# State-space layer: the skip term by ScalarE and an identity product, a modulation unit in halves about the input products

## The reference, cut to what matters

```python
u = (xn @ w_in).astype(jnp.float32)
...
y = (jnp.einsum('ghp,blgp->blgh', c_re.astype(jnp.float32), xr)
     - jnp.einsum('ghp,blgp->blgh', c_im.astype(jnp.float32), xi))
y = y.reshape(B, L, D_MODEL) + d_skip.astype(jnp.float32) * u
hg = jax.nn.gelu(y).astype(xn.dtype) @ w_glu
```

## Time and profile before

| | us |
|---|---|
| median of 3 runs | 1801.25 |
| lowest, highest | 1799.35, 1802.07 |
| the profiled execution, its own time | 1802.3 |
| its span in the trace | 1800.5 |
| clock granted to TensorE, mean | 0.978 |

### The profile page before, as it was taken

How to read it: one execution, slowest core, us unless ns; L and a number is a source line. 1 busy time by engine, 2 the same in 40 slices (tenths; PEclk the granted TensorE clock), 3 DMA queues, 4 the chain that set the end, 5 groups by cost and what they waited for, 6 DMA issues and landing times.

```text
span 1800.5 us, 34542 instructions
## 1 busy us (share of the span) xinstructions
PE 1689.0 (94%) x14415; PEld 1600.2 (89%) x14429; DVE 1238.5 (69%) x1567; ACT 844.9 (47%) x964; POOL 156.1 (9%) x128
## 2 busy tenths in 40 slices
PE   6999999998899997799999999999999999989997
PEld 6979999898899985599999897999998658889997
DVE  5847777786887757867777784777776667555454
ACT  5355545546445441245555535555544633343343
POOL 1002000103920043100000100200000000000000
PEclk9999999899999989999999999999999999999999
DMA  7804545535345531353554680445452032044551
GB/s 297 333 13 164 178 181 183 188 133 187 141 173 177 186 118 72 142 209 142 183 184 182 230 334 19 167 173 188 175 187 94 24 117 94 25 156 174 185 184 70
DMA packets 40050, 286.50 MB, mean 159 GB/s; under 512 B 4576, under 2 KB 4576, under 8 KB 5664
## 3 DMA queue, kind: packets, MB, share of 16 engines
q1 hardware_dynamic: 39024, 280.99, 43.1%
q10 hardware_dynamic: 944, 4.33, 0.6%
HBM read 284.25 MB, written 1.05 MB: 158 GB/s over the span
## 4 chain that ended last, share of the span: by engine, by line
PE 65%; DVE 17%; ACT 9%; issue 6%; POOL 1%; DMA 1%; DVEq 0%; ACTq 0%; POOLq 0%; SPq 0%
PE PS L1770 19%; PE PS L1771 19%; PE PS L1772 19%; ACT whi L386 5%; DVE wlo L928 4%; DVE AR L1153 4%; ACT AR L498 1%; DVE AR L1264 1%; DVE AR L1261 1%; ACT AR L589 1%; ACT AR L591 1%; DVE XL L972 1%; PE PS L2374 1%; POOL AR L2533 1%; DVE AR L1139 1%
## 5 line engine op out<-in xcount | busy, mean ns | idle before, releaser
L1770 PE MATMUL PS<-XH,whi 128*128 128x256 f32 (+1 forms) x2696 | 787.6, 292 | 46.8 <-DVE wlo L928 35.0
L1771 PE MATMUL PS<-XL,whi 128*128 128x256 f32 (+1 forms) x2696 | 778.4, 289 | 0.0
L1772 PE MATMUL PS<-XH,wlo 128*128 128x256 f32 (+1 forms) x2696 | 778.0, 289 | 0.0
L928 DVE TENSOR_TENSOR wlo<-raw,whi 128x2048 fp32r<-128x2048 f32 x240 | 557.3, 2325 | 180.7 <-ACT whi L386 180.6
L1770 PEld LDWEIGHTS PS<-XH,whi 128*128 128x128 f32 x2696 | 522.0, 194 | 60.6 <-issue 29.5
L1771 PEld LDWEIGHTS PS<-XL,whi 128*128 128x128 f32 x2696 | 522.7, 194 | 4.4 <-issue 0.2
L1772 PEld LDWEIGHTS PS<-XH,wlo 128*128 128x128 f32 x2696 | 522.5, 194 | 4.2
L386 ACT ACTIVATE whi<-raw 128x2048 fp32r<-128x2048 f32 x240 | 456.0, 1902 | 72.4 <-PE PS L1772 47.9
L1770 PE MATMUL PS<-HH,whi 128*128 128x256 f32 x880 | 250.7, 285 | 13.0 <-DVE HL L1173 8.5
L1772 PE MATMUL PS<-HH,wlo 128*128 128x256 f32 x880 | 249.7, 284 | 0.0
L1771 PE MATMUL PS<-HL,whi 128*128 128x256 f32 x880 | 249.7, 284 | 0.0
(11 more groups left out here) (365 smaller groups left out, 1522.5 us busy)
## 6 DMA issues: line engine op xcount, KB each, us to landing
raw<-wst SPq DMA_DIRECT2D x248, 1024.0 KB, 4.8
AR<-mst SPq DMA_DIRECT2D x17, 1024.0 KB, 5.5
XT<-x_in SPq DMA_DIRECT2D x2, 512.0 KB, 6.2
AR<-crow ACTq DMA_DIRECT2D x2, 512.0 KB, 5.7
AR<-sbc ACTq DMA_DIRECT2D x1, 1024.0 KB, 5.8
AR<-ctxin ACTq DMA_DIRECT2D x1, 1024.0 KB, 5.6
y_out<-XT SPq DMA_DIRECT2D x1, 1024.0 KB, 3.9
AR<-sgw ACTq DMA_DIRECT2D x1, 512.0 KB, 3.6
```

The source lines that it names most:

```text
L928: dve.tensor_tensor(wlo[:, r, :], raw[:, u % RING, :], whi[:, r, :].bitcast(F32), ALU.subtract)\
L1770: pe.matmul(dst, sh, mh, start=first, stop=False, **kw)
L1771: pe.matmul(dst, sh, ml, start=False, stop=False, **kw)
L1772: return pe.matmul(dst, sl, mh, start=False, stop=last, **kw)
```

## The change

The additions of DVE (`outputs(b)`, L1448) are removed. In their place ACT scales the two blocks of `U5` in place (Copy with the skip's column as scale, 128x256) once the first of the pair's two output steps is done, and signals `u5_skip`. In the second of the two steps PE waits for that and adds the scaled blocks to the bank with two products with the identity, in full precision, ahead of the 128 passes. ACT's gelu reads the bank itself and writes `U5`. What waited for `y5_sum` now waits for `gelu5`. DVE's wait for `y5_ready` 8 stays ahead of `modulation_rows`. In steps 1, 3 and 5 PE runs the first four of the modulation unit's eight matmuls, then the inputs, then the other four.

```diff
--- before.py
+++ after.py
@@ -286,7 +286,7 @@
                  "gss_ready", "grms_ready", "grstd_ready", "gvn_ready", "mix_ready", "gs_ready", "gtril",
                  "gy_ready", "glu_sig", "glu_mul", "link", "s5_step", "s5_dt", "s5_den", "s5_bt", "s5_set", "s5_c2", "s5_k0", 
                  "s5_angle", "s5_table", "s5_xb", "s5_turned", "s5_b", "bu_ready", "bu_mult",
-                 "v_ready", "scan_ready", "rot_ready", "x5_ready", "jump", "jump_parts", "y5_ready", "y5_sum",
+                 "v_ready", "scan_ready", "rot_ready", "x5_ready", "jump", "jump_parts", "y5_ready", "u5_skip",
                  "gelu5", "silu_c", "scp_nil", "mod_rows", "mod_sum", "mod_vec", "ctx_in", "mod_gain",
                  "c_in", "c_row", "x5_last", "ctx_rms", "ctx_inv", "ctx_diag", "ctx_row", "gains2", "second", "second_rms", "row_diag", "row_twice", "ml_in0", "ml_in1", "ml_used",
                  "normed", "wide_taken", "csq", "csum", "crms", "crinv", "cnormed", "kv_part", "q_out", "rot",
@@ -676,9 +676,15 @@
                 silu_c(1)
                 t.u += MODS[0][1]
                 for b in range(4):
-                    act.wait_ge(S["y5_sum"], b + 1)
+                    act.wait_ge(S["y5_ready"], 2 * b + 1)
+                    for k in (2 * b, 2 * b + 1):
+                        a = act.activation(U5[:, k, :], U5[:, k, :], ACT.Copy, scale=vcol("ssm_d", k))
+                    a.then_inc(S["u5_skip"], 1)
+                    act.wait_ge(S["y5_ready"], 2 * b + 2)
                     y = U5[:, 2 * b:2 * b + 2, :]
-                    act.activation(y, y, ACT.Gelu_apprx_tanh).then_inc(S["gelu5"], 1)
+                    act.activation(y.rearrange("p k (c e) -> p k c e", e=2),
+                                   PS[:, 4 + b % 2, :].rearrange("p (k e c) -> p k c e", k=2, e=2), ACT.Gelu_apprx_tanh)\
+                        .then_inc(S["gelu5"], 1)
                     act.wait_ge(S["gelu5"], b + 1)
                     act.activation(XH[:, 2 * b:2 * b + 2, T:2 * T], y, ACT.Copy).then_inc(S["op_hi"], 1)
                     if b == 2:
@@ -1439,15 +1445,6 @@
                         dve.tensor_tensor(JRE[:, c8], JA[:, c8], JB[:, c8], ALU.subtract).then_inc(S["jump"], 1)
                         dve.tensor_tensor(JIM[:, c8], JC[:, c8], JD[:, c8], ALU.add).then_inc(S["jump"], 1)
 
-                def outputs(b):
-
-                    dve.wait_ge(S["y5_ready"], 2 * b + 2)
-                    for kk in range(2):
-                        u5 = U5[:, 2 * b + kk, :].rearrange("p (c e) -> p c e", e=2)
-                        y5 = PS[:, 4 + b % 2, kk * T:(kk + 1) * T].rearrange("p (e c) -> p c e", e=2)
-                        ins = dve.scalar_tensor_tensor(u5, u5, vcol("ssm_d", 2 * b + kk), y5, ALU.mult, ALU.add)
-                    ins.then_inc(S["y5_sum"], 1)
-
                 def lows(b):
                     low(XL[:, 2 * b:2 * b + 2, T:2 * T], U5[:, 2 * b:2 * b + 2, :], XH[:, 2 * b:2 * b + 2, T:2 * T],
                         t.op + b + 1)
@@ -1455,11 +1452,11 @@
                 for s in range(8):
                     products(s)
                     scans(s)
-                    if s >= 2:
-                        (lows if s % 2 else outputs)(s // 2 - 1)
+                    if s >= 2 and s % 2:
+                        lows(s // 2 - 1)
                 split_lo(t.s)
                 t.s += 1
-                outputs(3)
+                dve.wait_ge(S["y5_ready"], 8)
                 dve.wait_ge(S["w_used"], sum(MODS[0]))
                 modulation_rows(0, 7)
                 lows(3)
@@ -1777,15 +1774,16 @@
             def x(k, a=0, b=T):
                 return XH[:, k, a:b], XL[:, k, a:b]
 
-            def modulation(g, bank):
+            def modulation(g, bank, ks=range(KT)):
 
                 pe.wait_ge(w_loaded[t.u % RING], 16 * (t.u // RING + 1))
-                for k in range(KT):
+                for k in ks:
                     mm = pe.matmul(PS[32 * (g // 2):32 * (g // 2) + 32, bank, (g % 2) * 256:(g % 2) * 256 + 256],
                                    SCP[:, k, :], raw[:, t.u % RING, k * 256:(k + 1) * 256],
                                    start=(k == 0), stop=(k == KT - 1))
-                mm.then_inc(S["w_used"], 1)
-                t.u += 1
+                if k == KT - 1:
+                    mm.then_inc(S["w_used"], 1)
+                    t.u += 1
 
             def modulation_turned(n, bank):
 
@@ -2351,13 +2349,18 @@
                     kw = dict(skip_group_check=True)
                     if c == 0:
                         if b >= 2:
-                            pe.wait_ge(S["y5_sum"], b - 1)
+                            pe.wait_ge(S["gelu5"], b - 1)
                         pe.matmul(bank, ZB[:, 0:P], ZB[:, :], start=True, stop=False, **kw)
                         for kk in range(2):
                             for q in range(4):
                                 r = slice(32 * q, 32 * q + 32)
                                 pe.matmul(bank[r, kk * T:kk * T + P], K0T[r, 2 * b + kk, :], U5[r, 2 * b + kk, 0:T:2],
                                           start=False, stop=False, **kw)
+                    if c:
+                        pe.wait_ge(S["u5_skip"], b + 1)
+                        for kk in range(2):
+                            pe.matmul(bank[:, kk * T:(kk + 1) * T], ident,
+                                      U5[:, 2 * b + kk, :].rearrange("p (c e) -> p e c", e=2), start=False, stop=False, **kw)
                     pe.wait_ge(S["rot_ready"], s + 1)
                     if s < 7:
                         pe.wait_ge(S["x5_ready"], s + 1)
@@ -2380,10 +2383,13 @@
                 pe.wait_ge(S["silu_c"], 1)
                 for s in range(8):
                     if s % 2 and s < 7:
+                        modulation(s, 7, range(4))
                         inputs(s // 2 + 1)
-                    modulation(s, 7)
+                        modulation(s, 7, range(4, KT))
+                    else:
+                        modulation(s, 7)
                     if s == 7:
-                        pe.wait_ge(S["y5_sum"], 3)
+                        pe.wait_ge(S["gelu5"], 3)
                         begin(range(2), 2, T)
                     outputs(s)
                 begin(range(2, 6), 2, T)
```

## The result

| | before | after |
|---|---|---|
| median, us | 1800.17 (6 runs, 1799.13 to 1802.07) | 1807.95 (6 runs, 1804.88 to 1808.62) |
| ratio, 95% interval | | 1.0039 [1.0029, 1.0049] |
| profiled execution, its time and span | 1802.3, 1800.5 | 1808.0, 1806.2 |

The change makes the kernel slower by 0.39%, some 7 us (7.8 by the medians); 1804.3 us was forecast, with 1800.7 to 1806.2 as the range.

The account below looks back on a forecast made before the run. The scan was taken as bound by two nearly equal paths, DVE's and GpSimd with PE; 1.7 + 1.0 - 0.1 + 0.5 = +3.1 us on 1802.3 gave 1805.4, in medians 1804.3 us, range 1800.7 to 1806.2.

Parts of the forecast that it names:

- Step 2 is 1.7 us later by the half: Into step 2: DVE already waits for the inputs, so the half unit before them adds its whole length, +1.7 us.
- The page border lies 3 instructions into the half, and the page lands behind the unit's load: Into step 4: PE stops before nearly all of the half, awaiting instructions; the pair takes 18.8 us against 17.72, +1.0.
- T + 4.7: Into step 4: PE resumes 4.7 us after T, the end of GpSimd's products; the page lands at T + 2.3.
- the rival of the page without the load: Page's packet doesn't wait for the weight load, so it comes 1.2 us sooner: +1.2 in all, 1802.5 us; chance 0.15.
- the hidden fetch: Rival: no instruction page is late at the half; sum about +0.2, 1801.5 us; chance 0.20.
- Steps 4 to 6, -0.1: Into step 6: the half runs before the page border in the inputs; the pair takes 17.1 us against 17.25.
- The clock stays up at the gap: PE's clock stays at 1.00 through the instruction-page gap, as in one trace; no clock term in the sum.
- my third rival: Page-border gap lowers PE's clock; half, inputs, next half and outputs cost up to 3 us more: +6, 1807 us; chance 0.12.
- The end, +0.5: After step 6: DVE's 0.78 us lost to waiting for ScalarE's scaling, identity products +0.87, removed last addition gives 0.3 back.
- The profiled execution of before as base: The +3.1 us was added to the profiled execution's 1802.3 us, taken as 1.05 above the median.

Follow-up runs that it names:

- the halves alone: Kernel before with only the modulation unit split about the inputs, DVE still adding the skip: ratio 1.0018 [1.0009, 1.0027].
- 40 waits: Changed kernel plus 40 already-met stand-alone wait instructions in PE's queue in step 0, to move page borders: 1809.01 us, ratio 1.0047.
- the skip's path alone: Changed kernel with the modulation unit whole again, behind the inputs: 1810.94 us, ratio 1.0058 [1.0045, 1.0071].

## Why the prediction was wrong

- *Step 2 is 1.7 us later by the half:* right. +1.6 by the means, +2.0 in the experiment that had the halves alone.
- *The page border lies 3 instructions into the half, and the page lands behind the unit's load:* right. The gap follows the first pass of the half, and at equal clock the pair took 18.82 where 18.8 was worked out. PE resumed 4.6 us after GpSimd's end (716.28 to 711.66), with T + 4.7 in the forecast and T + 3.5 in the rival of the page without the load. So this rival falls, and the hidden fetch too. (The latter's terms add up to +0.1 and not +0.2, which changes nothing.)
- *Steps 4 to 6, -0.1:* right, -0.15 by the means.
- *The clock stays up at the gap:* **the step that failed.** I took "in the gap of 2.42 us it stayed at 1.00" from one trace as the rule for this stage, and the sum has nothing for the clock. Over four traces of each kernel it fell at or just behind the gap in one before and in three after, for 1.3 to 1.7 us each. Steps 2 to 4 so became 2.2 us longer by the means, where +1.0 was in the sum. The clock was my third rival, put at 0.12 and at +3 us for this place; it came about more often, and at half the size. That its 1807 us lies near the measured 1807.95 is luck in part. The falls in step 0's inputs (+0.8 by the means, the code up to there is the same) are the other missing part. Whether the change makes either fall more frequent stays open: the numbers of traces are too small.
- *The end, +0.5:* right in three traces, wrong in one. The three took 29.5 to 29.6 us against 28.92 in three of before, +0.6 to +0.7: the 12 products ran at half clock, as assumed, and the identity products waited for ScalarE. In the first trace the 12 products ran at full clock after 3.48 us of idle time and left PE waiting 2.03 us, and the clock fell for the last outputs: +2.2. The mean is +0.8. An identity pair took 1.10 us from its first start to the next line's (760.88 to 761.98), not 0.87.
- *The profiled execution of before as base:* its part ahead of the scan was 2.5 to 4.3 us longer than in the three others (start of the stage 682.10 against 677.83 to 679.55), and its scan was one of the fastest. So one trace of each shows 6.4 us in the stage where the means show 5.2, and 5.7 us between the times where the medians of the result show 7.8. The median to which I added, 1801.25, was also 1.1 us above that of six runs, which brought the forecast nearer to the result than its +3.1 us was.

By the means, 5.2 of the 6.2 us between the spans are in the stage. The 1.05 us in the rest stays open.

## What to carry to other kernels

Before a step is put in front of work that another engine waits for, ask what released that work last; if it was the engine's own queue, the step costs its length. Where PE runs many small products, count the instructions to the page border: a few inserted instructions decide whether the page is asked for before or behind a weight load, and a saving elsewhere shows only when no page is late. Waits put in to move a border cost time themselves (0.11 us each here) and fit only where the engine idles longer than that. A single profile of a kernel with stalls near 2 us does not tell what the clock does in them: take several before putting a chance on it.

## What the runs showed of the hardware that I had not expected

- The granted clock does not fall at the same place in each execution. The same gap in the same kernel was crossed at 1.00 in the first and at 0.58 in the second trace of the kernel before (length, busy, clock, DMA share, GB/s of the stretch behind it; 59 passes of inputs took 3.42 us in place of 2.08):

```profile
714.80:718.20 3.40, 3.40 (x60) 0.58 0.02 5
```

- In every gap by "issue" of 1.8 us and more inside a run of PE's products (not those that the waits make ahead of the outputs), the page's packet left within 0.4 us of the end of a 1 MB load, and PE resumed 2.2 to 2.5 us after the packet started. The stall was 1.8 to 3.6 us there, and only 0.28 where work of the old page was left (step 6 of the changed kernel). Where the packet came ahead of the load, as in steps 2 to 4 with 40 waits, there was none. The rule of the Trainium skill ("DMA: Bandwidth & Descriptors", "Queues, rings and completion order") that a DMA engine alternates between queues by packet would let the page through. At these gaps the trace does not agree: the packet left at the load's end. It is no rule for all loads: in the fourth trace of before a packet of q8 started between 756.1 and 756.3, inside a load that lasted from 754.6 to 759.2. The DMA queues in the changed kernel's trace, three stretches of 0.25 us from 713.50, 713.75 and 714.00 (packets, MB, time taken as a share of 16 engines' span):

```profile
q1 hardware_dynamic: 14, 0.09, 85.7%
...
q14 instruction: 1, 0.01, 7.7%
q1 hardware_dynamic: 6, 0.00, 1.4%
...
q8 instruction: 1, 0.02, 23.7%
q1 hardware_dynamic: 6, 0.00, 1.4%
```

  The load's large packets have all started by 713.75, the page's packet (q8) follows at 714.0, and PE resumes at 716.28. In the skip's path alone the packet stands in the stretch from 712.00 and PE resumes at 714.46; with 40 waits ahead, from 730.75 and at 733.27.
- A weight load does not always take the same time. In the skip's path alone ScalarE began on the third unit 6.4 us after that unit's last product (754.96 to 761.37), not 4.65; the fourth unit's load had been issued 2.9 us behind it. That the two loads share the DMA engines is likely but not shown: with 40 waits ahead a second load was issued 1.75 us behind the first, which landed after 4.8 us, and in the kernel before a load took 6.05 us (issued at 756.25, landed at 762.30) with no other in flight.
